# Output projection with features in the partitions, a gate column in place of a broadcast gate, and work moved ahead of the expert selection

## What is computed

```python
hn = rmsnorm(x) * (1 + scale1) + shift1          # scale1, shift1, gate1, ... = silu(c) @ w_mod
proj = hn @ w_in
merge = sigmoid(proj[..., OFF_MERGE:] + b_merge)
y_pool, y_rwkv = ...                             # pooling branch, two-way RWKV-7 scan
mixed = (merge[:D] * y_pool + merge[D:] * y_rwkv) @ w_o
x = x + gate1 * mixed                            # the residual x1
hn2 = rmsnorm(x) * (1 + scale2) + shift2
x = x + gate2 * moe(hn2)                         # 32 experts, the 4 best of each token
y = rmsnorm(x)
```

## Time and profile before

| | us |
|---|---|
| median of 3 runs | 1229.28 |
| lowest and highest | 1229.22, 1230.01 |
| the profiled execution | 1230.77 |
| its span in the profile | 1229.0 |
| start of the first expert's products in it | 317.81 |
| busy: PE, DVE, ACT, POOL | 1185.6, 384.5, 195.0, 34.9 |

### The profile page before, as it was taken

How to read it: one execution, slowest core, us unless ns; L and a number is a source line. 1 busy time by engine, 2 the same in 40 slices (tenths; PEclk the granted TensorE clock), 3 DMA queues, 4 the chain that set the end, 5 groups by cost and what they waited for, 6 DMA issues and landing times.

```text
span 1229.0 us, 17191 instructions
## 1 busy us (share of the span) xinstructions
PE 1185.6 (96%) x6971; PEld 556.3 (45%) x6971; DVE 384.5 (31%) x854; ACT 195.0 (16%) x361; POOL 34.9 (3%) x78
## 2 busy tenths in 40 slices
PE   6999999999999999999999999899999999999997
PEld 3777889988333333333333333333333333333334
DVE  3577894363412111112211211321112122121112
ACT  2340223201311111111111111111111112111102
POOL 3000110120000000000000000000000000000000
PEclk9999999999999999999999999999999999999999
DMA  9999312499999999999999999999999999999995
GB/s 366 338 329 308 110 53 93 147 390 389 402 427 429 429 428 428 428 430 428 428 427 429 429 406 429 428 427 429 430 428 427 427 429 429 428 428 428 429 430 219
DMA packets 67752, 464.34 MB, mean 378 GB/s; under 512 B 8151, under 2 KB 31342, under 8 KB 41726
## 3 DMA queue, kind: packets, MB, share of 16 engines
q1 hardware_dynamic: 64560, 458.11, 90.5%
q0 software_dynamic: 1504, 4.75, 1.0%
q10 hardware_dynamic: 1646, 0.86, 0.2%
HBM read 462.37 MB, written 1.34 MB: 377 GB/s over the span
## 4 chain that ended last, share of the span: by engine, by line
PE 73%; DMA 25%; DVE 1%; issue 0%; SPq 0%; ACT 0%; DVEq 0%
PE bank L1390 28%; DMA ring<-in_expert_w_gu 23%; PE bank L1460 11%; PE sums L721 5%; PE sums L742 4%; PE sums L1488 3%; PE bank L1302 3%; PE sums L1194 2%; PE sums L1267 2%; DMA ring<-in_w_mod 2%; PE bank L1339 2%; PE sums L664 1%; PE sums L866 1%; PE bank L1429 1%; PE bank L1330 1%; PE bank L1069 1%
## 5 line engine op out<-in xcount | busy, mean ns | idle before, releaser
L1390 PE MATMUL bank<-ring,gate 128*64 128x512 f32 x1992 | 443.9, 601 | 18.3 <-DMA ring<-in_expert_w_gu 18.3
L1390 PEld LDWEIGHTS bank<-ring,gate 128*64 128x64 f32 x1992 | 140.7, 138 | 317.3 <-issue 286.0
L1460 PE MATMUL bank<-ring,gate 128*64 128x512 f32 x960 | 212.6, 595 | 2.8
L2325 DVE TENSOR_SCALAR gate<-bank 128x512 f32<-128x512 f32 x32 | 22.1, 692 | 371.6 <-PE bank L1390 371.6
L1460 PEld LDWEIGHTS bank<-ring,gate 128*64 128x64 f32 x960 | 68.4, 137 | 126.3 <-issue 125.9
L1833 ACT ACTIVATE corr<-gate 128x512 f32<-128x512 f32 x32 | 20.1, 629 | 646.6 <-DVE gate L2325 646.6
L2351 DVE TENSOR_TENSOR corr<-bank,spare 128x512 f32<-128x512 f32 x31 | 21.4, 692 | 221.7 <-PE bank L1460 221.7
L1488 PE MATMUL sums<-corr,kk 64*128 64x512 f32 x248 | 61.6, 615 | 0.0
L1302 PE MATMUL bank<-bt,vt 128*64 128x512 f32 x256 | 60.4, 592 | 0.0
L721 PE MATMUL sums<-hnT,ring 128*128 128x256 f32 x256 | 56.4, 380 | 0.0
L742 PE MATMUL sums<-hnT,ring 128*128 128x256 f32 x240 | 55.5, 386 | 0.0
(11 more groups left out here) (429 smaller groups left out, 995.3 us busy)
## 6 DMA issues: line engine op xcount, KB each, us to landing
ring<-in_expert_w_gu SPq DMA_DIRECT2D x123, 2048.0 KB, 18.9
ring<-in_expert_w_down SPq DMA_DIRECT2D x62, 2048.0 KB, 19.0
ring<-in_w_mod SPq DMA_DIRECT2D x24, 1024.0 KB, 10.9
ring<-in_w_in SPq DMA_DIRECT2D x17, 1024.0 KB, 10.0
ring<-in_w_o SPq DMA_DIRECT2D x3, 1024.0 KB, 8.5
ring<-in_expert_w_gu SPq DMA_DIRECT2D x3, 1024.0 KB, 13.8
more<-in_expert_w_down SPq DMA_DIRECT2D x2, 1024.0 KB, 7.2
ring<-in_w_pool_out SPq DMA_DIRECT2D x2, 1024.0 KB, 5.0
```

The lines of the kernel that those rows point to most:

```text
L1390: last = mm(b[h * SLOTS:(h + 1) * SLOTS, :], xg[:, 2 * (u % 2) + i, u // 2, :], w(u, i, j, h), start=False, stop=(u == GU_UNITS - 1 and i ...
L1460: last = mm(DN[h * SLOTS:(h + 1) * SLOTS, :], actT[:, i, u, :], w(GU_UNITS + u, i // 2, i % 2, h), start=(u == 0 and i == 0), stop=(u == D ...
```

## The change

Seven edits, all made together:

1. The projection has weights stationary (128x128 blocks of `w_o`) and both token halves of `ms` moving, so results have features in the partitions. Eight groups, one for each block k of 128 features, alternate between banks 5 and 6. The gate is a column of `modb`, and one DVE operation for each token half gives `x1T[k]` at once. `gbc` and its two broadcasts are gone, `gcol`, `grow` and `scratch` have three parts.
2. For that x must be feature-major: TensorE turns x at the front ahead of `xn` (16 transposes into banks 1 to 4), and ACT copies it into x's own memory (`xT`), once `xn` is made. The turns of `xn` into a bank wait for that copy.
3. `x1_turn(k)` turns `x1T[k]` back into `sums` (token-major), two transposes in the middle of the next group. `start_sums` is gone. ACT's squares and DVE's scaling by `scale2` read `sums` in three pieces (512, 384, 128 columns of each half).
4. SP's list: `once_half(4, 1)` is issued right behind `expert_unit(0, 3)`; `once_half(2, 0)` still waits for `r2`; `once_half(3, 1)` waits for the residuals and `once_half(0, 0)` for the last logits.
5. ACT's copy of the logits stands ahead of its root. DVE's first `x2_part` stands ahead of the logits, the second behind the selection.
6. The biases of the gate half and one filler product of 512 columns stand ahead of the wait for the selection; the other half's biases stay behind it.
7. The first one-hot is made in two halves of 64 columns; the gather waits for the first ones only.

```diff
@@ sync
+        once_half(4, 1)
         sp.wait_ge(S("rout_mm"), 4)
         expert_unit(0, 5)
...
         once_half(4, 0)
-        sp.wait_ge(S("wo_used"), 8)
-        once_half(4, 1)
         sp.wait_ge(S("late_dve"), DONE["r2"])
         once_half(2, 0)
-        sp.wait_ge(S("late_mm"), AFTER["sums"])
+        sp.wait_ge(S("wo_used"), NS * KT)
         once_half(3, 1)
+        sp.wait_ge(S("lgT_mm"), 1)
         once_half(0, 0)
@@ gpsimd
-            pool.dma_start(gbc[:, s, :], scratch[0, s:s + 1, :].to_broadcast([P, D])).then_inc(S("gbc_in"), 16)
@@ tensor
+        pe.wait_ge(S("x_in"), 32)
+        for k in range(KT):
+            for s in range(NS):
+                last = tr(banks[1 + k // 2][:, (k % 2) * TT + s * T:(k % 2) * TT + (s + 1) * T], x[:, s, k * P:(k + 1) * P], ident[:])
+        last.then_inc(S("front_mm"), 1)
...
             for k in range(KT):
+                if s == 0 and k % 2 == 0:
+                    pe.wait_ge(S("xT_ready"), k // 2 + 1)
                 b = banks[1 + k // 2]
...
+        def x1_turn(k):
+            for s in range(NS):
+                pe.wait_ge(S("wo_used"), NS * k + s + 1)
+                if k == KT - 1:
+                    pe.wait_ge(S("sq_done"), 2 + 3 + s)
+                    pe.wait_ge(S("x2_scaled"), 4)
+                mm(sums[:, 2 * s + k // 4, (k % 4) * T:(k % 4 + 1) * T], x1T[k][:, s * T:(s + 1) * T], ident[:], is_transpose=True,
+                   start=(k % 4 == 0), stop=True, skip_group_check=True).then_inc(S("x1t_mm"), 1)
...
+        for k in range(KT):
+            c, o = k // 2, (k % 2) * P
+            if k == 6:
+                pe.wait_ge(S("tiles_in"), 32)
+            elif k % 2 == 0:
                 arrived(pe, AT["WO", c])
+            if k >= 2:
+                pe.wait_ge(S("wo_used"), NS * (k - 1))
+            for i in range(KT):
+                if k == 0:
+                    pe.wait_ge(S("rout_used"), i + 1)
+                w = ring_in(AT["WO", c])[:, i, o:o + P] if c < 3 else wo3[i // 4][:, i % 4, o:o + P]
+                last = mm(banks[5 + k % 2][:, 0:TT], w, ms[:, i, :], start=(i == 0), stop=(i == KT - 1))
+                if k and i == 3:
+                    x1_turn(k - 1)
+            last.then_inc(S("wo_mm"), 1)
...
+        pe.wait_ge(S("bgu_in"), 64)
+        pe.wait_ge(S("sele_ready"), 1)
+        up_bias(G, 0)
+        mm(banks[7][:, :], ident[:], ones[:].unsqueeze(1).to_broadcast([P, 4, P]), start=True, stop=True)
 
         pe.wait_ge(S("late_dve"), DONE["sel"])
@@ scalar
+        act.wait_ge(S("front_mm"), AFTER["xT"])
+        act.wait_ge(S("xn_ready"), NS)
+        for j in range(4):
+            af(xT[:, 2 * j:2 * j + 2, :].rearrange("p k t -> p (k t)"), banks[1 + j][:, :], ACT.Copy).then_inc(S("xT_ready"), 1)
...
+        for r, (h, c0, c1, turned) in enumerate(sums_parts):
+            for s in range(NS):
+                act.wait_ge(S("x1t_mm"), NS * (turned - 1) + s + 1)
+                if s and r < 2:
+                    act.wait_ge(S("x2_scaled"), 2 * r + 1)
+                act.wait_ge(S("sq_done"), 2 + NS * r + s)
+                af(vt[:, 0, 0:c1 - c0], sums[:, 2 * s + h, c0:c1], ACT.Square, accum_out=sqp[:, s, r:r + 1]).then_inc(S("sq_done"), 1)
+        act.wait_ge(S("lgT_mm"), 1)
+        af(lgT, banks[4][:, 0:T], ACT.Copy).then_inc(S("lgT_ready"), 1)
         act.wait_ge(S("late_dve"), DONE["sqsum"])
         af(stat[:, 6:8], stat[:, 4:6], ACT.Sqrt, bias=epsr[:], scale=1.0 / D).then_inc(S("rms2_ready"), 1)
-        act.wait_ge(S("lgT_mm"), 1)
-        af(lgT, banks[4][:, 0:T], ACT.Copy).then_inc(S("lgT_ready"), 1)
@@ vector
+        dve.wait_ge(S("xT_ready"), 4)
+        for k in range(KT):
+            dve.wait_ge(S("wo_mm"), k + 1)
             for s in range(NS):
+                ts = slice(s * T, (s + 1) * T)
+                v.scalar_tensor_tensor(x1T[k][:, ts], banks[5 + k % 2][:, ts], modb[:, 0, k, s:s + 1], xT[:, k, ts], MUL, ADD).then_inc(S("wo_used"), 1)
+            if k == 3:
                 dve.wait_ge(S("mod_in"), 64)
+            if k in (3, 6):
+                r = k // 6
+                dve.wait_ge(S("x1t_mm"), NS * (k + 1))
+                x2_scale(r, 1).then_inc(S("x2_scaled"), 1)
+                dve.wait_ge(S("sq_done"), 2 + NS * r + 1)
+                x2_scale(r, 0).then_inc(S("x2_scaled"), 1)
...
-        choose(0, 0)
-        x2_part(1, 0)
+        for s in range(NS):
+            last = v.tensor_scalar(p2[:, s, 0:SLOTS], iota2[:, 0:SLOTS], base[:, 0:1], rank[:, s, 0:1], ADD, ALU.is_equal)
+        last.then_inc(S("sel_ready"), 1)
```

## The result

The changed kernel takes 1231.61 us (median of 22 executions, 1228.83 to 1234.68) beside 1229.57 for the kernel before (22, 1228.35 to 1230.89). The ratio is 1.0018, 95% interval 1.0012 to 1.0024: within 0.2%, at its upper edge. That is +2.0 to +2.2 us where the sum gave +0.4, and 0.1 us under the 1231.7 from which the prediction counted it as slower. A second measurement on another chip gave 1.0015 (1.0006 to 1.0024).

A forecast was written before the change was run, and what follows sets the result against it. TensorE bounds up to the first expert, then the full-rate transfers. MiB -2.45, projection +0.6, gap +0.05, front +2.2 sum to +0.4 us on the median 1229.28: forecast 1229.7 us, range 1226.9 to 1232.2.

The forecast's parts named there:

- What bounds the kernel: Behind the first expert TensorE goes at the transfers' pace, 428 GB/s; an earlier first expert alone is worth nothing.
- The MiB, -2.45: Half unit issued at 262.61 instead of 307.70, ahead of the transfer pause, shortens the stream behind it: -2.45 us.
- Rival (D): The MiB lengthens the stream before 305 as much as it shortens it behind; gain 0 to 2.45, 1230.9 us; chance 0.03.
- The broadcasts at nothing: Removing the two gate broadcasts frees 2.7 us before 305, but that is lost in the pause: no gain.
- The projection, +0.6: Output projection: transposes and logit steps among the products take 2.59 us for 2.02, so the last product is 0.6 later.
- The gap at `r2`, 0.05: Behind the output projection the next transfer comes just in time after the one MiB: gap 0.05 us, up to 1.0.
- Rival (C): Norm's chain after the last output product holds the transfers waiting at `r2`, up to 2.1 us: 1231.8 us; chance 0.13.
- The front, +2.2: Turning x first delays the modulation product, its last piece by 2.6 us, less 0.4 given back: +2.2 us, passed on whole.
- The pace of the row: Front transposes take 0.225 us each, twice the 0.11 elsewhere; this slow value was taken, product starting at 17.7.
- No fall of the clock followed at 29 us: Without the wait before the last modulation piece, the clock fall behind it goes: 0.4 us given back.
- The selection, 0.8 sooner: Between output projection and first expert the logits chain shortens: first expert perhaps 0.8 us sooner, worth nothing but cover.
- Its worth as cover: Half units last until about 324.4; the refill by expert 0 must be issued before 322.5 and is at 320.9.

The follow-up runs named there:

- experiment 8: Changed kernel with filler in the selection's gaps, plus the half unit into `prc` moved back behind the last residual: 1232.39 us, 1.0021 to the kernel before.
- mib_late: Changed kernel with the half unit into `prc` issued behind the last residual, as before the change: 1231.87 us, 1.0026 to the kernel before.
- after: The changed kernel itself, all seven edits against the kernel before, first measurement and its trace: 1231.61 us, 1.0018.
- experiment 5: Kernel before without the two gate-row broadcasts, `scale2` standing in for the gate; it made 33 expert passes instead of 32: 1259.18 us, 1.0239.
- after_again: The changed kernel, nothing altered, measured and traced a second time: 1231.77 us, 1.0015 to the kernel before.
- filler_first: Changed kernel with six unread products of 512 columns ahead of the first transpose: 1232.69 us, 1.0031 to the kernel before.
- experiment 6: Also written `gaps_filled`: changed kernel with three unread products of 256 columns in TensorE's selection gaps: 1230.66 us, 1.0002 to the kernel before.
- front_in_product: Changed kernel with selection gaps filled, and x turned in four batches within the modulation product, replacing its fillers: 1230.25 us, 1.0003 to the kernel before.
- all_three: Changed kernel with gaps filled, x turned in the modulation product, and three quarters of x's half unit fetched early; measured twice: 1229.05 us (0.9995), 1229.6 us (0.9997).
- x_early: Changed kernel with three quarters of the half unit into x issued two groups earlier, ahead of the pause: 1229.95 us, 1.0000 to the kernel before.

## Why the prediction was right, and where it was not

The change is within 0.2%, to which I had given 0.73, and the time, 1.9 us above the 1229.7 forecast, lies within the range. But it lies near the upper edge, only 0.1 us on this side of "slower", so luck had a part in it; and one step was wrong.

- **What bounds the kernel: right behind the first expert.** TensorE waits for weights 12 times still, 17.8 us, and a MiB ahead of the pause is worth its time at 428 GB/s. That an earlier first expert is worth nothing did not hold for the changed kernel; see the last point.
- **The MiB, -2.45: right, 2.3** (experiment 8). Rival (D), that the broadcasts had run in gaps so that the MiB would gain less, gave a mean gain of 1.2; the first measurement, 1.4, was near it, the second is not, though its interval (0.8 to 3.9) reaches there. The traces speak against (D): from the first expert on, four with the MiB behind the pause take 912.1 us on average, eight with it ahead 909.9, and ahead of that the MiB costs nothing: from the branch output to the first expert it is 55.3 in `mib_late` as in `after`.
- **The broadcasts at nothing: supported**, by the empty queue of experiment 5 more than by its time.
- **The projection, +0.6: 0.8.** From the first product of the branch output ahead of it (L1194 before, L1200 after) to the last of the output projection it is 44.69 us in the kernels with the old form and 45.46 in all with the new one. A pair of transposes costs the 0.22 that I gave it; the other 0.2 I did not trace.
- **The gap at `r2`, 0.05: right.** From `kt_` (309.85) to `qr` (312.33) SP waits 2.48 us; 2.5 was forecast. Rival (C), which needed this chain to be over 2.45 by microseconds, is out.
- **The front, +2.2: near, and too high by the traces.** The slow turn costs 1.2 to 1.6 in them, the quick one 0.1 or nothing; the kernel with the front alone has 1.85 in the median, whose traced execution had the quick turn. The pace of the row was the right one to take, but it is one of two. No fall of the clock followed at 29 us, as forecast (it came earlier, at 15.3): the four transposes there take 0.72 us for 0.99. The 0.4 that I gave back for it was a little much; it is 0.3 by the distance from the last piece to the first projection product (3.84 for 4.12).
- **The selection, 0.8 sooner: 0.5.** The way from the end of the output projection to the first expert went from 11.06 to 9.81 us, less the 0.8 by which the projection grew.
- **Its worth as cover: wrong.** This is the step that failed. I had the half units last until 324.4 and the refill issued at 320.9, with 1.6 us to spare before 322.5. The 324.4 has no sum behind it: five half units take 12.2 us at 428 GB/s, and from the issue at 307.4, with the 1.9 us to the first bytes that I allowed the refill, they last until 321.6. Only six, as in the kernel before, come near 324. On that scale (the last product at 307.4, in the trace 2.45 later) the refill was issued at 321.0. But five MiB, 5.24 MB, wait behind the pause. Summed from the windows of `after`, second by second from 310, they are spent at 324.9, 322.5 on that scale: 1.9 us sooner than I said. A transfer issued onto the idle stream shows its first bytes after about 1.0 us (the half unit issued at 309.85, and the refill at 326.05 of `after_again`), but the bytes that follow add up as if the full rate had begun after 1.8. For the refill that is 325.3. So the cover is not 1.6 us but about -0.4, and the second dip, which loses 0.5 us from 325 to 327, is just that. In the kernel before six MiB, 6.29 MB, are spent at 324.1 by the same sum, with the refill there at 323.5: 0.6 of cover. The change took one MiB of backlog out of the stretch and did not shorten the way to the refill by as much, so that TensorE, not the transfers, now sets when the stream is full again. The traces with the MiB ahead show it without any sum: whether the first expert starts at 316.63 or at 322.21, 909.4 to 910.3 us follow (911.3 in `filler_first`), so here its start goes into the time almost whole.

Two things follow. The missing cover costs about 0.5 us in an execution whose clock holds. And it lets through what would have been absorbed in part: the fall of the clock in the selection. In `after_again` the way from the projection to the first expert took 3.7 us more than in `after`; with 1.1 less ahead of it and 0.4 less behind, the span is 2.2 us longer. The 10 of 33 executions with the low mean clock are 2.65 us longer than the others, +0.8 in the mean. Forecast +0.4, cover +0.5, clock +0.8: +1.7, where the 33 executions average 2.2 us over those of the kernel before beside them. The 0.5 between is within the intervals, but it is no proof of the sum: the +0.4 still has the front at 2.2, and with 1.2 to 1.6, as the slow traces show it, 0.6 to 1.0 more is unexplained. With filler in the gaps the whole is +0.25 by experiment 6 (-0.9 to +1.35), which the forecast of +0.4 fits, and so would +0.9. So it is shown that the gaps cost 1.6 to 2.0 us, with an interval of 1.3 to 1.6 either way; how they do, beyond the 0.8 of the low mean clock, is open.

The gaps were there to be foreseen. I had counted `start_sums` as work that leaves a chain. The timeline of the kernel before shows that it also kept TensorE busy between short products, and experiment 6 that filler in these places brings the time back; I noticed the clock only at the front.

**Open.** Why `front_in_product` is no faster than `gaps_filled`, although its traced front is 1.8 us shorter: a difference of 1.5 us between them is just outside what the two intervals allow, and both measurements of `all_three` lean the same way. A possibility, not tried, is that the quick turn is more frequent in `gaps_filled` than its one trace says; then there is little left to gain. Another is the fall of the clock, since two executions of `front_in_product` have the low mean. Why `filler_first` is 0.16% over `after_again` is open too.

## What to carry to other kernels

Where a stream pauses and is taken up by a refill, write down both times, when the backlog behind the pause is spent and when the refill brings the stream back to its full rate, from the same windows: a byte moved ahead of the pause gains its time only as long as the first is the later one. Work that a change removes from a chain of short products may have been what kept the clock up; look for the gaps that it leaves, and fill them, even though the filler shortens nothing on the path. And one trace shows one case: read the mean clock of all executions before explaining a median.

## What was unexpected of the hardware

- **Short gaps, a long fall, and not always.** Gaps of 0.45 and 0.47 us, between products of 0.4 to 0.6, were followed by 10 us at a granted clock of 0.50 in `after_again`; the same gaps in `after` by none. 10 of 33 executions have the low mean clock, 6 of 10 with a hole of 2.4 us, none of 11 with the gaps filled (2 of 55 over all kernels with the fillers). The Trainium skill ("TensorE: Matmul & The Clock Gate", Part 1) has the clock follow how busy TensorE has recently been, and says that at a kernel's start the number of slow products differs from run to run. The traces agree with both, and show the second in mid-kernel, at 312 us.
- **The same at the front.** With the same instructions, all sixteen transposes of `xn` took 0.22 to 0.25 us each in five traces; in three the second eight took 0.11 to 0.14. That moves the modulation product by 1.1 us (17.56, 16.45).
- **Two levels under one record.** The transposes of x at 9.02 run at 0.23 us each (twelve in 2.77), in `filler_first`, behind six products of filler, at 0.12 (twelve in 1.48). The clock column shows 1.00 for both at that place, and in `x_early` it still does at 16 us, where six transposes of `xn` take 1.49 us as they do at 0.50 in `after`. So at the front the pace tells the level and the column does not. The Trainium skill ("TensorE: Matmul & The Clock Gate", Part 4) says that the upper level does not engage for transposes. Here it did: behind filler twelve of them in a row kept the pace of the upper level.
